# Two attentions' projections in one stage, beside head norm and rotary work in two fp32r passes

## The chip, the cores and the metric

The kernel runs on one core of a Trainium2 chip. The metric is the device time of one execution in microseconds, the median of several runs. The engines are PE (TensorE, matrix multiplication; PEld is its weight load), DVE (VectorE), ACT (ScalarE), POOL (GpSimd) and SP (SyncE, which issues the loads of weights).

## What is computed

A hybrid model of two blocks on 512 tokens of width 1024, in float32. The first block mixes a state-space branch, an RWKV branch and an HGRN branch. The second block has two layers; each mixes four branches of width 512. Those that matter here:

```python
y_a = mlstm_branch(aq, ak, av, ao, ag, a_conv_w, a_gate_bias, a_norm_g)
y_b = gqa_branch(bq, bk, bv, b_qnorm_g, b_knorm_g)
y_c = natten_branch(cq, ck, cv, c_rpb)
y_d = diff_branch(dq, dk, dv, d_lq1, d_lk1, d_lq2, d_lk2, d_subln_g, lambda_init)
...
# end of mlstm_branch, per head of 128
h = (h - mu) * lax.rsqrt(var + EPS)
h = h * norm_g
return h * jax.nn.sigmoid(o)
...
# gqa_branch: 8 query heads and 2 key heads of 64
q = rms_norm(q, qn_g); k = rms_norm(k, kn_g)
q = axial_rope(q, ang_r, ang_c) * (B_DH ** -0.5)
k = axial_rope(k, ang_r, ang_c)
```

Branch D ends with a norm over heads of 128 too, and so does HGRN in the first block.

## The kernel before

Activations lie transposed: 128 features on the partitions, 512 tokens along them, a matrix of 1024 features as 8 tiles. A product in float32 accuracy is made of three fp32r passes (`three_passes`, lines 555 to 557): weight and activation are each split into a high part, rounded to fp32r, and a low part, the rest. Weights stream in chunks of at most 128x1024. For every chunk SP loads it (four slots ahead), ACT makes its high part (L478), DVE its low part (L484), both into two slots, and PE multiplies. `run_ahead` makes ACT and DVE prepare chunk p+2 as soon as PE has used chunk p.

The program is a row of stages. Each is one `nc.Block()` with a stream for each engine, and no engine enters the next stage before all have left the last (the branches at L882 or L1338 are such borders). `project` multiplies k.xn by a list of weight matrices; ACT takes each finished tile out of PSUM (L1000), and for a tokens job four tiles at the end (L1008). Work of another kind runs beside it: a side object has one generator per engine, and `next(side_pieces)` runs its next piece behind each chunk, on PE right behind the chunk's matmuls, on ACT and DVE ahead of the preparation for the chunk after. What is left at the end runs in `list(side_pieces)`. `Together` advances two sides at once.

Per layer three stages stand in a row: the mLSTM's (branch A), then `project` of B's q, k, v (6 tiles) with `HeadNorm` of A beside it, then `project` of D's q, k (8 tiles) and v (four token chunks) with `DiffSetup` (lambda, a distance bias on POOL) and `Rotary` (norm and rotation of B's q and k) beside it. Behind them comes `project_beside` for C.

`HeadNorm` works on tile m: PE sums the tile with a matrix of ones (L3286) for the mean if it centres, DVE subtracts (L3322), ACT squares (L3306), PE sums the squares (L3293), ACT takes Sqrt (L3312), DVE the reciprocal (L3328), and multiplies by weight and inverse (L3332), then by the gate (L3336). `Rotary` squares (L3834), sums over pairs of 64 (L3860), Sqrt (L3839), reciprocal (L3880), scaling (L3882), a matmul with the turning matrix (L3866), three DVE operations with sine and cosine (L3887 to L3890), and at the end doubles the keys (L3871, L3850). All these constant matmuls are plain fp32: 8 per layer in A's norm, 12 in the rotary work, 4 per layer in D's norm (beside the mixing of C, in `gated_products`, where gate chunks are 1024 wide and value chunks 512), and 4 in HGRN's norm (beside `w_mix_ssm`, with chunks of 1024 alone). That makes 52.

## Time and profile before

| | us |
|---|---|
| median of 3 runs (3898.14 to 3909.04) | 3904.27 |
| the profiled execution | 3907.71 |
| its span, first to last instruction | 3905.5 |
| PE busy | 3674.9 (94%) |
| DVE busy | 2036.4 (52%) |
| ACT busy | 1528.7 (39%) |
| mean granted clock of TensorE | 0.969 |

The span is divided by engine: busy is time with an instruction at work. PE's matmul records overlap, so the distance from one start to the next is what a matmul costs, not its own length. The granted clock is the share of 2.4 GHz that TensorE got, 0.5 being 1.2 GHz.

### The profile page before, as it was taken

The numbers are of one execution on the slowest core, as the hardware profiler recorded it, in microseconds if no ns is written. First come the engines' busy times: TensorE is split into PE (matmuls) and PEld (weight loads), VectorE is DVE, ScalarE is ACT, GpSimd is POOL, SyncE is SP. The second block draws the span as 40 slices with busy tenths as digits, with TensorE's granted clock in tenths as the row PEclk, the third lists the DMA queues.
The fourth block names the chain that finished last, engine by engine and source line by source line (L and its number), as shares of the span: only waits on it lengthen the run. The fifth ranks groups of instructions, "written<-read, shape, count | busy, mean of one in ns | idle before, by whom it ended". The sixth has DMA issues, their size and how long they took to land. (4 is left out here: it accounts for less than half of the span.)

```text
span 3905.5 us, 51947 instructions
## 1 busy us (share of the span) xinstructions
PE 3674.9 (94%) x20468; PEld 2855.8 (73%) x20468; DVE 2036.4 (52%) x3128; ACT 1528.7 (39%) x2404; POOL 400.5 (10%) x353
## 2 busy tenths in 40 slices
PE   7898889969999999889999999999889999999998
PEld 5456777758878887666777788887666777788887
DVE  4879665584443334656545553333565555544332
ACT  4464432543343334333444333323433454333322
POOL 0018233000011110310000001100010000001100
PEclk9899989979999999999999999999999999999999
DMA  3011001203232232112212232232212112232232
GB/s 111 22 41 60 7 2 61 71 12 120 90 100 97 97 95 84 49 52 67 68 49 99 88 105 94 97 96 88 65 40 74 56 59 98 86 103 92 97 95 78
DMA packets 83486, 289.31 MB, mean 74 GB/s; under 512 B 9168, under 2 KB 9296, under 8 KB 82000
## 3 DMA queue, kind: packets, MB, share of 16 engines
q1 hardware_dynamic: 82848, 283.68, 22.7%
q8 instruction: 142, 2.33, 0.2%
q10 hardware_dynamic: 432, 2.78, 0.2%
q14 instruction: 64, 0.52, 0.0%
HBM read 284.32 MB, written 2.10 MB: 73 GB/s over the span
## 5 line engine op out<-in xcount | busy, mean ns | idle before, releaser
L484 DVE TENSOR_TENSOR weights_lo_r<-raw_weights,weights_hi_r 128x1024 fp32r<-128x1024 f32 (+2 forms) x554 | 639.4, 1154 | 1310.7 <-ACT weights_hi_r L478 1310.4
L478 ACT ACTIVATE weights_hi_r<-raw_weights 128x1024 fp32r<-128x1024 f32 (+2 forms) x554 | 547.1, 988 | 1396.6 <-PE ps L557 1323.1
L556 PE MATMUL ps<-xn_r,weights_hi_r 128*128 128x512 f32 x2688 | 1057.3, 393 | 0.0
L555 PE MATMUL ps<-xn_hi,weights_hi_r 128*128 128x512 f32 x1632 | 681.6, 418 | 65.6 <-PEq L882 23.4
L557 PE MATMUL ps<-xn_hi,weights_lo_r 128*128 128x512 f32 x1632 | 646.7, 396 | 0.0
L556 PEld LDWEIGHTS ps<-xn_r,weights_hi_r 128*128 128x128 f32 x2688 | 511.9, 190 | 112.7 <-issue 12.0
L555 PE MATMUL ps<-y_r,weights_hi_r 128*128 128x512 f32 x1200 | 473.8, 395 | 8.0 <-DVE weights_lo_r L484 5.9
L557 PE MATMUL ps<-y_r,weights_lo_r 128*128 128x512 f32 x1200 | 470.0, 392 | 0.0
L555 PEld LDWEIGHTS ps<-xn_hi,weights_hi_r 128*128 128x128 f32 x1632 | 313.0, 192 | 168.2 <-issue 82.9
L557 PEld LDWEIGHTS ps<-xn_hi,weights_lo_r 128*128 128x128 f32 x1632 | 312.3, 191 | 69.0
L555 PEld LDWEIGHTS ps<-y_r,weights_hi_r 128*128 128x128 f32 x1200 | 227.3, 189 | 61.3 <-issue 13.2
L557 PEld LDWEIGHTS ps<-y_r,weights_lo_r 128*128 128x128 f32 x1200 | 227.4, 190 | 47.6
L555 PE MATMUL ps<-y_hi,weights_hi_r 128*128 128x512 f32 x576 | 230.4, 400 | 2.1 <-PEq L1126 1.9
L557 PE MATMUL ps<-y_hi,weights_lo_r 128*128 128x512 f32 x576 | 224.7, 390 | 0.0
L556 PE MATMUL ps<-y_r,weights_hi_r 128*128 128x512 f32 x528 | 209.2, 396 | 0.0
L555 PE MATMUL ps<-hidden_hi,weights_hi_r 128*128 128x512 f32 x528 | 206.4, 391 | 1.0 <-PEq L4210 1.0
L557 PE MATMUL ps<-hidden_hi,weights_lo_r 128*128 128x512 f32 x528 | 205.5, 389 | 0.0
L556 PE MATMUL ps<-hidden_r,weights_hi_r 128*128 128x512 f32 x528 | 205.5, 389 | 0.0
L1483 POOL TENSOR_TENSOR y<-y 128x512 f32<-128x512 f32 x18 | 23.3, 1293 | 1674.6 <-ACT y L1472 1674.6
L4307 POOL TENSOR_TENSOR y<-y 128x512 f32<-128x512 f32 x63 | 81.3, 1291 | 611.7 <-ACT y L4264 611.7
L555 PEld LDWEIGHTS ps<-y_hi,weights_hi_r 128*128 128x128 f32 x576 | 108.2, 188 | 29.6 <-issue 4.0
L557 PEld LDWEIGHTS ps<-y_hi,weights_lo_r 128*128 128x128 f32 x576 | 108.1, 188 | 23.1
(552 smaller groups left out, 5224.9 us busy)
## 6 DMA issues: line engine op xcount, KB each, us to landing
raw_weights<-in_w_ffn_dram SPq DMA_DIRECT2D x132, 512.0 KB, 3.7
raw_weights<-in_w_down_dram SPq DMA_DIRECT2D x48, 512.0 KB, 3.5
raw_weights<-in_w_out_dram SPq DMA_DIRECT2D x24, 512.0 KB, 3.5
raw_weights<-in_w_down_dram SPq DMA_DIRECT2D x24, 384.0 KB, 3.1
raw_weights<-in_w_hgrn_dram SPq DMA_DIRECT2D x16, 512.0 KB, 3.5
raw_weights<-in_w_mix_ssm_dram SPq DMA_DIRECT2D x16, 512.0 KB, 3.7
raw_weights<-in_w_a_qk_dram SPq DMA_DIRECT2D x16, 512.0 KB, 3.5
raw_weights<-in_w_mix_a_dram SPq DMA_DIRECT2D x16, 512.0 KB, 3.5
```

The lines of the kernel that those rows point to most:

```text
L478: act.activation(self.k.w_hi[:, g % 2, 0:chunk.width], self.k.raw[:, slot, 0:chunk.width], ACT.Copy)\
L484: dve.tensor_tensor(self.k.w_lo[:, g % 2, 0:chunk.width], self.k.raw[:, slot, 0:chunk.width], self.k.w_hi[:, g % 2, 0:chunk.width].bitcast ...
L555: pe.matmul(out, w_hi, x_hi, start=start, stop=False)
L556: pe.matmul(out, w_hi, x_lo, start=False, stop=False)
L557: return pe.matmul(out, w_lo, x_hi, start=False, stop=stop)
L1483: pool.tensor_tensor(self.sums[:, n, :], self.sums[:, n, :], self.sq[:, kinds * (m % 2) + n, :], ALU.add)\
L4307: pool.tensor_tensor(gate[:, s, :], gate[:, s, :], rstd, ALU.mult).then_inc(gate_scaled, 1)
```

## The change

- `two_passes` takes the place of the fp32 matmuls with constants: the constant is exact in fp32r, the other operand is split into high and low part, and two fp32r matmuls add up. Constants are rounded once by ACT copies (`sums_r`, `consts_r`).
- In `HeadNorm` and `Rotary` ACT squares twice (float32 and rounded to fp32r) and DVE subtracts the two; where y or q and k are the operand, ACT copies the high part and DVE subtracts.
- Sqrt and DVE's reciprocal become Ln and Exp(-0.5 x) on ACT, in place.
- A's norm is a piece later where it centres (`late`).
- B's and D's projections are one `project`, with A's norm, the rotary work (from piece 6 on, keys first) and `DiffSetup` (from piece 1 on) beside it. The rotary work uses the norm's buffers; its tensor side waits for the norm's last root before its first piece.
- A's gate o lies in y_b, and not in a buffer of its own.

```diff
+        act.wait_ge(self.more_in, 16)
+        at = k.rounded("turn", "dup")
+        act.activation(k.consts_r[:, at], k.consts[:, at], ACT.Copy)
...
+def two_passes(pe, out, exact, hi, lo):
+    pe.matmul(out, exact, hi, start=True, stop=False)
+    return pe.matmul(out, exact, lo, start=False, stop=True)
...
 class HeadNorm(Nothing):
...
     def tensor(self, pe):
+        k, w = self.k, self.work
+        for p in range(self.tiles + 2 + self.late):
+            m = p - self.late
+            if self.centre and 0 <= m < self.tiles:
+                pe.wait_ge(self.part_lo, m + 1)
+                if m >= 2:
+                    pe.wait_ge(self.centred, m - 1)
+                two_passes(pe, bank(k.ps, 4 + m % 2), self.over, w.hi[:, m % 2, :], w.lo[:, m % 2, :])\
+                    .then_inc(self.mean_done, 1)
+            m = p - 2 - self.late
+            if m >= 0:
+                pe.wait_ge(self.square_lo, m + 1)
+                if m >= 2:
+                    pe.wait_ge(self.root, m - 1)
+                two_passes(pe, bank(k.ps, 6 + m % 2), self.over, w.sq_hi[:, m % 2, :], w.sq_lo[:, m % 2, :])\
+                    .then_inc(self.summed, 1)
+            yield
...
     def scalar(self, act):
+        if self.rounds:
+            act.activation(k.sums_r[:, :], k.consts[:, k.rounded("ones", "pair")], ACT.Copy)
+        for p in range(self.tiles + 2 + self.late):
             m = p
             if self.centre and m < self.tiles:
                 if m >= 2:
-                    pe.wait_ge(self.centred, m - 1)
-                pe.matmul(bank(k.ps, 4 + m % 2), self.over, self.y[:, m, :], start=True, stop=True)\
-                    .then_inc(self.mean_done, 1)
-            m = p - 2
-            if m >= 0:
-                pe.wait_ge(self.squared, m + 1)
-                if m >= 2:
-                    pe.wait_ge(self.root, m - 1)
-                pe.matmul(bank(k.ps, 6 + m % 2), self.over, self.sq[:, m % 2, :], start=True, stop=True)\
-                    .then_inc(self.summed, 1)
-            yield
-
-    def scalar(self, act):
-        k = self.k
-        for p in range(self.tiles + 2):
-            m = p - 1
+                    act.wait_ge(self.mean_done, m - 1)
+                act.activation(w.hi[:, m % 2, :], self.y[:, m, :], ACT.Copy).then_inc(self.part_hi, 1)
+            m = p - 1 - self.late
             if 0 <= m < self.tiles:
                 if self.centre:
                     act.wait_ge(self.centred, m + 1)
                 if m >= 2:
                     act.wait_ge(self.summed, m - 1)
-                act.activation(self.sq[:, m % 2, :], self.y[:, m, :], ACT.Square).then_inc(self.squared, 1)
-            m = p - 2
+                act.activation(w.sq[:, m % 2, :], self.y[:, m, :], ACT.Square).then_inc(self.squared, 1)
+                act.activation(w.sq_hi[:, m % 2, :], self.y[:, m, :], ACT.Square).then_inc(self.squared, 1)
+            m = p - 2 - self.late
             if m >= 0:
+                rt = w.rt[:, m % 2, :]
                 act.wait_ge(self.summed, m + 1)
                 if m >= 2:
                     act.wait_ge(self.scaled, m - 1)
-                act.activation(self.rt[:, m % 2, :], bank(k.ps, 6 + m % 2), ACT.Sqrt, bias=self.eps,
+                act.activation(rt, bank(k.ps, 6 + m % 2), ACT.Ln, bias=self.eps,
                                scale=1.0 / (self.head * self.factor * self.factor)).then_inc(self.root, 1)
+                act.wait_ge(self.root, m + 1)
+                act.activation(rt, rt, ACT.Exp, scale=-0.5).then_inc(self.inverse, 1)
             yield
     def vector(self, dve):
+        for p in range(self.tiles + 3 + self.late):
+            m = p - self.late
+            if self.centre and 0 <= m < self.tiles:
                 dve.wait_ge(self.mean_done, m + 1)
                 dve.scalar_tensor_tensor(out=self.y[:, m, :], in0=bank(k.ps, 4 + m % 2), scalar=-1.0 / self.head,
                                          in1=self.y[:, m, :], op0=ALU.mult, op1=ALU.add).then_inc(self.centred, 1)
-            m = p - 3
+            m = p
+            if self.centre and m < self.tiles:
+                dve.wait_ge(self.part_hi, m + 1)
+                dve.tensor_tensor(w.lo[:, m % 2, :], self.y[:, m, :], w.hi[:, m % 2, :].bitcast(F32), ALU.subtract)\
+                    .then_inc(self.part_lo, 1)
+            m = p - 1 - self.late
+            if 0 <= m < self.tiles:
+                dve.wait_ge(self.squared, 2 * m + 2)
+                dve.tensor_tensor(w.sq_lo[:, m % 2, :], w.sq[:, m % 2, :], w.sq_hi[:, m % 2, :].bitcast(F32),
+                                  ALU.subtract).then_inc(self.square_lo, 1)
+            m = p - 3 - self.late
             if m >= 0:
-                rt = self.rt[:, m % 2, :]
-                dve.wait_ge(self.root, m + 1)
-                dve.reciprocal(rt, rt).then_inc(self.inverse, 1)
                 dve.wait_ge(self.inverse, m + 1)
                 if self.centre:
                     dve.wait_ge(self.centred, m + 1)
                 dve.scalar_tensor_tensor(out=self.y[:, m, :], in0=self.y[:, m, :], scalar=k.col(self.weight, m),
-                                         in1=rt, op0=ALU.mult, op1=ALU.mult).then_inc(self.scaled, 1)
+                                         in1=w.rt[:, m % 2, :], op0=ALU.mult, op1=ALU.mult).then_inc(self.scaled, 1)
...
 class Rotary(Nothing):
+    ORDER = (4, 0, 1, 2, 3)
...
     def scalar(self, act):
+        act.wait_ge(self.before.summed, self.before.tiles)
+        act.wait_ge(self.before.scaled, self.before.tiles - 1)
+        for p in range(self.pieces):
+            i, odd = divmod(p, 2)
+            if odd and i < N:
+                rt, key = w.rt[:, i % 2, :], self.ORDER[i] == 4
+                act.wait_ge(self.summed, i + 1)
+                if i < 2:
+                    act.wait_ge(self.before.scaled, self.before.tiles)
+                else:
+                    act.wait_ge(self.roped, 3 * (i - 1))
+                act.activation(rt, bank(k.ps, 4 + i % 2), ACT.Ln,
+                               bias=k.const("eps")[:, 0:1] if key else k.const("eps")[:, 3:4],
+                               scale=1.0 / 64 if key else 1.0).then_inc(self.root, 1)
+                act.wait_ge(self.root, i + 1)
+                act.activation(rt, rt, ACT.Exp, scale=-0.5).then_inc(self.inverse, 1)
+                if i == 0:
+                    act.wait_ge(self.v_turned, 1)
+                    act.activation(self.v_tok, bank(k.ps, 7).rearrange("p (j f) -> p j f", j=NT), ACT.Copy)\
+                        .then_inc(self.v_taken, 1)
...
     def tensor(self, pe):
+        pe.wait_ge(self.before.root, self.before.tiles)
+        pe.wait_ge(self.before.centred, self.before.tiles)
+        pe.wait_ge(self.tile_used, 6)
         for j in range(NT):
-            mm = pe.transpose(k.ps[:, 6, j * P:(j + 1) * P], self.v[:, j * P:(j + 1) * P], k.const("ident"))
+            mm = pe.transpose(k.ps[:, 7, j * P:(j + 1) * P], self.v[:, j * P:(j + 1) * P], k.const("ident"))
         mm.then_inc(self.v_turned, 1)
         yield
-        for m in range(5):
-            pe.wait_ge(self.squared, m + 1)
-            pe.matmul(bank(k.ps, 4 + m % 2), k.const("pair"), self.sq[:, m % 2, :], start=True, stop=True)\
-                .then_inc(self.summed, 1)
-            yield
-            pe.wait_ge(self.normed, m + 1)
-            if m == 0:
-                pe.wait_ge(self.v_taken, 1)
-            pe.matmul(bank(k.ps, 6 + m % 2), k.const("turn"), self.qk[:, m, :], start=True, stop=True)\
-                .then_inc(self.rotated, 1)
-            yield
-        pe.wait_ge(self.roped, 15)
-        for g in range(2):
-            pe.matmul(bank(k.ps, 4 + g), k.const("dup")[:, g * P:(g + 1) * P], self.qk[:, 4, :],
-                      start=True, stop=True).then_inc(self.doubled, 1)
+        for i in range(N + 1):
+            if i < N:
+                pe.wait_ge(self.square_lo, i + 1)
+                two_passes(pe, bank(k.ps, 4 + i % 2), k.const_r("pair"), w.sq_hi[:, i % 2, :], w.sq_lo[:, i % 2, :])\
+                    .then_inc(self.summed, 1)
+            if i:
+                pe.wait_ge(self.part_lo, i)
+                if i == 2:
+                    pe.wait_ge(self.v_taken, 1)
+                two_passes(pe, bank(k.ps, 6 + (i - 1) % 2), k.const_r("turn"), w.hi[:, (i - 1) % 2, :],
+                           w.lo[:, (i - 1) % 2, :]).then_inc(self.rotated, 1)
+            if i == N:
+                pe.wait_ge(self.root, N)
+                pe.wait_ge(self.part_lo, N + 1)
+                for g in range(2):
+                    two_passes(pe, bank(k.ps, 4 + g), k.const_r("dup")[:, g * P:(g + 1) * P], w.hi[:, N % 2, :],
+                               w.lo[:, N % 2, :]).then_inc(self.doubled, 1)
...
 def layer_branches(k, n, y, y_lo, early, product, opening):
...
+    o_gate = y_b
+    mlstm_branch(k, n, y_a, o_gate, norm, opening)
+    c_qk = k.sbuf(window, "c_qk", [P, 8, T], "right")
+    b_qk = k.sbuf(grouped_qkv, "b_qk", [P, 5, T], "right")
+    b_k2 = k.sbuf(grouped_qkv, "b_keys_twice", [P, 2, T], "right")
+    b_v = k.sbuf(grouped_qkv, "b_v", [P, NT, P], "right")
+    d_qk = k.sbuf(d_parts, "d_qk", [P, 8, T])
+    d_v = k.sbuf(d_parts, "d_v", [P, NT, 512])
+    lam, slope = k.sbuf(d_parts, "lambda", [P, 8]), k.sbuf(d_parts, "distance_bias", [P, D_HEADS, 896])
+    with ExitStack() as work:
+        v = k.sbuf(work, "b_v_rows", [P, 1, T], "right")
+        norm_a = HeadNorm(y_a, A_HEADS, P, f"a_norm{n}", k.const("eps")[:, 0:1], o_gate, centre=True)
+        rotary = Rotary(n, b_qk, b_k2, v[:, 0, :], b_v[:, :, :], 6, norm_a)
+        project(k, [(f"w_b_q{n}", b_qk[:, 0:4, :], 1.0), (f"w_b_k{n}", b_qk[:, 4:5, :], 1.0), (f"w_b_v{n}", v, 1.0),
+                    (f"w_d_q{n}", d_qk[:, 0:4, :], 0.125), (f"w_d_k{n}", d_qk[:, 4:8, :], 1.0)], k.xn,
+                tokens=(f"w_d_v{n}", d_v), beside=Together(Together(norm_a, rotary), DiffSetup(n, lam, slope)))
```

How the instructions stand now at three places. ACT beside A's norm in layer 0, one chunk's worth (L1000 or L1009 takes a tile, L478 or L487 makes a weight's high part), before:

```order
L478 ACTIVATE weights_hi_r_50<-raw_weights 128x1024 [waits chunk_used,weights_in_2]
L1000 ACTIVATE b_qk<-ps 128x512 [waits chunk_used]
L3306 ACTIVATE head_norm_work<-y 128x512 [waits e_ready_2071,ssm_scaled_3786]
L3312 ACTIVATE head_norm_work<-ps,consts 128x512 [waits e_ready_2071]
L478 ACTIVATE weights_hi_r_50<-raw_weights 128x1024 [waits chunk_used,weights_in_3]
```

The same place now:

```order
L487 ACTIVATE weights_hi_r_50<-raw_weights 128x1024 [waits chunk_used,weights_in_2]
L1009 ACTIVATE b_qk<-ps 128x512 [waits chunk_used]
L3339 ACTIVATE parts_hi<-y 128x512 [waits tile_used_7029]
L3346 ACTIVATE squares<-y 128x512 [waits tokens_used_7030]
L3347 ACTIVATE squares_hi<-y 128x512
L3354 ACT_TABLE_LOAD
L3354 ACTIVATE roots<-ps,consts 128x512 [waits sig_ready_7025]
L3357 ACT_TABLE_LOAD
L3357 ACTIVATE roots<-roots 128x512 [waits f_ready_7026]
L487 ACTIVATE weights_hi_r_50<-raw_weights 128x1024 [waits chunk_used,weights_in_3]
```

Five more instructions stand between two weight parts, two of them table loads.

PE at the border between B's and D's projections in layer 0, before:

```order
L557 MATMUL ps<-xn_hi,weights_lo_r_51 128x512
L3293 MATMUL ps<-head_norm_work,consts 128x512 [waits factor_ready_2072,ssm_normed_3787]
L882 UNCONDITIONAL_BRANCH
L924 UNCONDITIONAL_BRANCH [waits barrier_Pool_Activation_PE_DVE_SP_release]
L555 MATMUL ps<-xn_hi,weights_hi_r_50 128x512 [waits parts_ready]
```

Now (f_ready_7026 is the semaphore that the norm's Ln counts up):

```order
L566 MATMUL ps<-xn_hi,weights_lo_r_51 128x512
L3289 MATMUL ps<-squares_hi,sums_r 128x512 [waits f_ready_7026,exped_7024]
L3290 MATMUL ps<-squares_r_14623,sums_r 128x512
L3938 MATMUL ps<-consts,b_v_rows 128x128 [waits rest_ready_8006,tokens_used_7030,f_ready_7026]
L3938 MATMUL ps<-consts,b_v_rows 128x128 x3
L564 MATMUL ps<-xn_hi,weights_hi_r_50 128x512 [waits parts_ready,rest_ready_8006]
```

The border is gone; v is turned right behind the norm's last sum (which stands a chunk later than B's last tile), and waits for the norm's root.

ACT beside D's norm in layer 0, from one gate to the next, before:

```order
L1058 ACTIVATE gate<-ps 128x512 [waits chunk_used]
L3306 ACTIVATE head_norm_work<-y 128x512
L3312 ACT_TABLE_LOAD
L3312 ACTIVATE head_norm_work<-ps,consts 128x512 [waits source_ready_164]
L478 ACTIVATE weights_hi_r_50<-raw_weights 128x512 [waits chunk_used,weights_in_0]
L3306 ACTIVATE head_norm_work<-y 128x512 [waits source_ready_164]
L3312 ACTIVATE head_norm_work<-ps,consts 128x512 [waits source_ready_164]
L478 ACTIVATE weights_hi_r_50<-raw_weights 128x1024 [waits chunk_used,weights_in_1]
L1058 ACT_TABLE_LOAD [waits dt_steps_173]
L1058 ACTIVATE gate<-ps 128x512 [waits chunk_used]
```

Now, from the 512 wide weight part on:

```order
L487 ACTIVATE weights_hi_r_50<-raw_weights 128x512 [waits chunk_used,weights_in_0]
L3346 ACTIVATE squares<-y 128x512 [waits scanned_176]
L3347 ACTIVATE squares_hi<-y 128x512
L3354 ACT_TABLE_LOAD
L3354 ACTIVATE roots<-ps,consts 128x512 [waits scanned_176]
L3357 ACT_TABLE_LOAD
L3357 ACTIVATE roots<-roots 128x512 [waits squared_166]
L487 ACTIVATE weights_hi_r_50<-raw_weights 128x1024 [waits chunk_used,weights_in_1]
L1067 ACTIVATE gate<-ps 128x512 [waits y_ready_1166,chunk_used]
L3346 ACTIVATE squares<-y 128x512 [waits scanned_176]
```

The gate (a Tanh) lost its table load, since Exp stands ahead of it; each of the two pieces between the gates got two.

## Rows read from the trace of the kernel before

**Rows 1.** The page's part 1: busy time, share of the span, instructions.

```profile
PE 3674.9 (94%) x20468; PEld 2855.8 (73%) x20468; DVE 2036.4 (52%) x3128; ACT 1528.7 (39%) x2404; POOL 400.5 (10%) x353
```

**Rows 2.** Windows, both layers' joined stretch: PE, PEld, DVE, ACT, POOL, clock, DMA, GB/s.

```profile
1682.70:1823.30 140.60, 122.94 (x478) 91.98 (x479) 74.21 (x62) 43.73 (x61) 10.88 (x4) 0.94 0.22 68
2874.50:3012.10 137.60, 121.32 (x479) 90.62 (x479) 73.76 (x62) 43.73 (x61) 9.80 (x4) 0.95 0.21 69
```

**Rows 3.** Timeline of PE, layer 0: start, length, instruction, idle before and releaser.

```profile
1721.79 1.02 PE L3293 MATMUL ps<-head_norm_work,consts 128*128 128x512 f32 x2
...
1732.67 0.77 PE L555 MATMUL ps<-xn_hi,weights_hi_r 128*128 128x512 f32 x1 [9.85 <-PEq L882]
...
1743.05 0.59 PE L4103 MATMUL ps<-lambda,consts 128*128 128x2 f32 x2 [3.27 <-DVE lambda L4092]
...
1760.48 1.13 PE L3866 MATMUL ps<-b_qk,consts 128*128 128x512 f32 x2 [1.81 <-DVE b_qk L3882]
```

**Rows 4.** Timeline of DVE while PE is idle at the border, layer 0.

```profile
1722.71 3.34 DVE L3328 RECIPROCAL head_norm_work<-head_norm_work 128x512 f32<-128x512 f32 x1
...
1727.49 3.34 DVE L3328 RECIPROCAL head_norm_work<-head_norm_work 128x512 f32<-128x512 f32 x1
...
1731.65 0.69 DVE L3336 TENSOR_TENSOR y<-y,o_gate 128x512 f32<-128x512 f32 x1
```

**Rows 5.** Timeline of PE around one fp32 sum (L3293), layer 0.

```profile
1715.22 0.39 PE L557 MATMUL ps<-xn_hi,weights_lo_r 128*128 128x512 f32 x1
1715.45 1.02 PE L3293 MATMUL ps<-head_norm_work,consts 128*128 128x512 f32 x2
...
1716.54 0.40 PE L556 MATMUL ps<-xn_r,weights_hi_r 128*128 128x512 f32 x1
```

**Rows 6.** Timeline of ACT, Ln (L4258) and Exp (L4261) of another stage.

```profile
1151.55 1.28 ACT L4258 ACT_TABLE_LOAD   x1
...
1153.55 1.28 ACT L4261 ACT_TABLE_LOAD   x1
...
1155.49 1.28 ACT L4264 ACT_TABLE_LOAD   x1
```

**Rows 7.** Timeline of ACT in one chunk beside A's norm, layer 0.

```profile
1709.46 0.58 ACT L1000 ACTIVATE b_qk<-ps 128x512 f32<-128x512 f32 x1
1709.94 0.62 ACT L3306 ACTIVATE head_norm_work<-y 128x512 f32<-128x512 f32 x1
1710.46 0.68 ACT L3312 ACTIVATE head_norm_work<-ps,consts 128x512 f32<-128x512 f32 x1
```

**Rows 8.** Timelines of PE and ACT beside D's norm, layer 1.

```profile
3343.98 0.47 PE L555 MATMUL ps<-xn_hi,weights_hi_r 128*128 128x512 f32 x1 [1.84 <-PEq L1338]
...
3371.52 1.12 PE L3293 MATMUL ps<-head_norm_work,consts 128*128 128x512 f32 x2
...
3381.60 0.47 PE L555 MATMUL ps<-xn_hi,weights_hi_r 128*128 128x512 f32 x1 [0.76 <-DVE weights_lo_r L484]
...
3358.00 1.06 ACT L478 ACTIVATE weights_hi_r<-raw_weights 128x1024 fp32r<-128x1024 f32 x1 [4.33 <-PE ps L557]
3358.97 0.58 ACT L1058 ACTIVATE gate<-ps 128x512 f32<-128x512 f32 x1
```

**Rows 9.** Timelines of PE and ACT at the end of D's projections, layer 0.

```profile
1819.46 1.88 PE L3871 MATMUL ps<-b_qk,consts 128*128 128x512 f32 x4
...
1821.59 1.12 ACT L3850 ACTIVATE b_keys_twice<-ps 128x512 f32<-128x512 f32 x2
...
1823.31 0.47 PE L555 MATMUL ps<-xn_hi,weights_hi_r 128*128 128x512 f32 x1 [1.97 <-PEq L882]
```

**Rows 10.** An idle of PE elsewhere, and windows behind three idles (clock third from the end).

```profile
1562.20 0.77 PE L555 MATMUL ps<-y_r,weights_hi_r 128*128 128x512 f32 x1 [2.96 <-DVE weights_lo_r L484]
...
1562.00:1569.00 7.00, 6.80 (x17) 5.38 (x18) 6.79 (x10) 0.00 (x0) 0.00 (x0) 0.55 0.27 75
1732.60:1739.60 7.00, 6.93 (x24) 5.49 (x24) 1.60 (x1) 1.06 (x1) 6.05 (x3) 0.79 0.50 150
1743.00:1753.00 10.00, 9.95 (x33) 7.88 (x33) 0.00 (x0) 0.99 (x3) 1.50 (x1) 0.69 0.19 52
```

More of the change, by code:

```diff
@@ L306, in const, with rounded, const_r @@
         return self.consts[0:rows, a:b]
+    def rounded(self, first, last):
+        return slice(self.const_at[first][0], self.const_at[last][1])
+    def const_r(self, name):
+        if name in ("ones", "pair"):
+            return self.sums_r[:, 0:P] if name == "ones" else self.sums_r[:, P:2 * P]
+        return self.consts_r[:, self.rounded(name, name)]
     def col(self, name, j=0, rows=P):
@@ L3261, with __init__ @@
+def two_passes(pe, out, exact, hi, lo):
+    pe.matmul(out, exact, hi, start=True, stop=False)
+    return pe.matmul(out, exact, lo, start=False, stop=True)
 class HeadNorm(Nothing):
-    def __init__(self, y, tiles, head, weight, eps, gate, factor=1.0, centre=False, work=None):
+    def __init__(self, y, tiles, head, weight, eps, gate, factor=1.0, centre=False, rounds=False):
+        self.work, self.rounds = None, rounds
         self.y, self.tiles, self.head, self.weight, self.eps = y, tiles, head, weight, eps
-        self.gate, self.factor, self.centre, self.work = gate, factor, centre, work
+        self.gate, self.factor, self.centre = gate, factor, centre
+        self.late = 1 if centre else 0
@@ L3270, in open @@
     def open(self, k, ctx):
         self.k = k
-        work = self.work if self.work is not None else k.sbuf(ctx, "head_norm_work", [P, 4, T])
-        self.sq, self.rt = work[:, 0:2, :], work[:, 2:4, :]
-        self.over = k.const("ones") if self.head == P else k.const("pair")
-        (self.mean_done, self.centred, self.squared, self.summed, self.root, self.inverse, self.scaled,
-         self.normed) = semaphores(k, ctx, "mean_done centred squared summed root inverse scaled normed")
-    def tensor(self, pe):
-        k = self.k
-        for p in range(self.tiles + 2):
+        self.work = NormWork(k, ctx, self.centre)
@@ new lines, in open @@
+        self.over = k.const_r("ones" if self.head == P else "pair")
+        (self.part_hi, self.part_lo, self.mean_done, self.centred, self.squared, self.square_lo, self.summed, self.root,
+         self.inverse, self.scaled, self.normed) = semaphores(
+            k, ctx, "part_hi part_lo mean_done centred squared square_lo summed root inverse scaled normed")
+    def tensor(self, pe):
+        k, w = self.k, self.work
[15 more added lines that the diff above has]
+            yield
@@ L3829, in scalar @@
     def scalar(self, act):
[L3830 to L3845 removed]
+        k, w, N = self.k, self.before.work, len(self.ORDER)
@@ L3852, in tensor @@
     def tensor(self, pe):
-        k = self.k
+        k, w, N = self.k, self.before.work, len(self.ORDER)
+        for _ in range(self.first):
+            yield
+        pe.wait_ge(self.before.root, self.before.tiles)
+        pe.wait_ge(self.before.centred, self.before.tiles)
+        pe.wait_ge(self.tile_used, 6)
         for j in range(NT):
-            mm = pe.transpose(k.ps[:, 6, j * P:(j + 1) * P], self.v[:, j * P:(j + 1) * P], k.const("ident"))
+            mm = pe.transpose(k.ps[:, 7, j * P:(j + 1) * P], self.v[:, j * P:(j + 1) * P], k.const("ident"))
@@ L4101, in tensor @@
     def tensor(self, pe):
+        for _ in range(self.FIRST):
+            yield
         pe.wait_ge(self.products, 1)
@@ L4109, in scalar @@
     def scalar(self, act):
+        for _ in range(self.FIRST):
+            yield
         act.wait_ge(self.dots, 1)
```

140 lines of the change are left out of this document (76 added, 64 removed).

## The prediction

> **What bounds the kernel now.** I read the busy shares first: TensorE (PE) works 94% of the span, no other engine above 52% [rows 1]. So a microsecond counts only if TensorE waits in it, runs at its lower clock, or works longer than it must. Then I looked at the two stages that the change joins, once per layer, from the first matmul of B's projections to the first of the stage behind D's: 140.5 us in layer 0 and 137.7 in layer 1 [rows 2]. TensorE is busy for 122.9 of the first 140.6.
>
> The timeline of TensorE around the border of the two stages says where the rest lies. B's last work there ends at 1722.8, and the next matmul begins at 1732.67: 9.85 us idle, with a branch (L882) as the releaser, which is a stage's end, not a tensor [rows 3]. VectorE's (DVE) own rows say what the stage's end waited for: three reciprocals of the head norm, 3.34 us each, the last behind 1727.49, and the gate product at 1731.65 [rows 4]. D's stage then idles 3.27 us more before the lambda matmul, since its first piece needs a product that VectorE makes late [rows 3]. After both idles TensorE runs at its lower level, 1.2 instead of 2.4 GHz: granted clock 0.79 over 7 us and 0.69 over 10 us [rows 10]. A stretch at mean clock c loses (1 - c) times its length: 1.5 and 3.1 us.
>
> **The change, part by part.**
>
> *Matmuls with constants.* An ordinary fp32r matmul of 512 columns takes 0.227 us from start to start. Between 1715.22 and 1716.54 stand two of these and one fp32 matmul with a constant, so the latter costs 1.32 - 0.45 = 0.87 [rows 5]. Two fp32r passes cost 0.46. Saved: 0.4 us for each of 52 such matmuls.
>
> *The joined stage, if TensorE never waited.* It issues 14 tiles of 24 matmuls and four token chunks of 24: 432 x 0.227 = 98.1 us. Seventeen pairs of passes (8 of norm A, 9 of the rotary work) add 7.8, lambda and the turning of v 0.65. The last rotation and the two doublings fall into the tail: in the kernel before, 3.85 us pass from the doublings' start (1819.46) to the next stage's first matmul, because ScalarE (ACT) takes out four tiles and then copies the doubled keys from 1821.59 [rows 9]. ScalarE has the same to do after the change, so 3.85 stays. Sum 110.4.
>
> *What ScalarE gets.* Instead of one Sqrt it now runs Ln and Exp for each tile, and the built program has a table load before each of them. The trace has this very sequence: load at 1151.55, next load at 1153.55, next at 1155.49, so a pair costs 3.94 us [rows 6]. Squares are made twice (0.52, and 0.64 if a load follows: 1.16), a tile is taken from PSUM in 0.48 [rows 7], a weight's high part in 0.96 [rows 8]. In chunks 3 to 5 ScalarE must do 0.96 + 0.48 + 1.16 + 3.94 = 6.5 us, in chunk 3 another 0.5 for the high part of y: 7.0. TensorE needs 24 x 0.227 plus one or two pairs, 5.9 to 6.4. ScalarE therefore falls behind.
>
> *Who waits for that.* Weight parts are made a chunk ahead, so a lag of 1 to 2 us there costs nothing. But the rotary piece behind chunk 6 makes TensorE wait for the fourth Ln of norm A before it turns v. With 0 at the first matmul, chunk 3 ends at 4 x 5.45 + 2 x 0.46 + 0.25 = 22.9, and chunk 6 with its sum at 42.0. ScalarE begins chunk 3's work at 23.2 and ends its rounds at 30.2, 36.7 and 43.2; then come high part, tile, table load and Ln: 0.96 + 0.48 + 2.0, to 46.6. TensorE waits 4.6 us. Behind TensorE's wait stands all of its queue: the next tile's 24 matmuls. Idles of 2.96, 3.27 and 9.85 us were each followed by the lower clock, costing 3.1, 3.1 and 1.5 us [rows 3, 10]; I take 2.3. The start of the rotary work (its first Ln waits for norm A's last scaling) costs perhaps 0.5. So the stage takes 110.4 + 4.6 + 2.3 + 0.5 = 117.8.
>
> *Stage gain.* 140.5 - 117.8 = 22.7 in layer 0, 137.7 - 117.8 = 19.9 in layer 1. The reciprocals go to nobody: VectorE gets subtractions of 0.7 us each for them, at most 4.6 us of a chunk, inside 6.
>
> *Norm D beside the mixing of C (once per layer).* A value chunk here has half the work, so the two chunks of a tile give TensorE only 8.2 us, against two pairs of Ln and Exp. With 0 at 3343.98, ScalarE starts the fifth weight part at 14.0 [rows 8]. Then: 0.96 + 0.48, squares 1.16, pair 3.94, to 20.5; 0.52, 1.16, 3.94, to 26.1; 0.96, 0.48 and the last squares 1.16, to 28.7; VectorE subtracts until 29.4. TensorE reached the fourth sum at 27.5 before (3371.52) and would reach it at 26.2 with three cheaper sums and a 0.17 us wait less. It waits 3.2 us. Without a fall of the clock the ninth chunk starts at 39.3, with it at 40.4; before it was 37.6 (3381.60). Cost 1.7 to 2.8 us, I take 2.5, twice: 5.0.
>
> *HGRN's norm.* Both chunks are full ones. ScalarE's last squares come out 0.2 us before TensorE wants them by the same working, so only the saving stays: 4 x 0.4 = 1.6. If that cover were missing it would cost about what a norm D costs.
>
> *Rest.* Rounding the constants (copies below 0.6 us on ScalarE, behind LoadX and in the first norm piece) lies beside full chunks: nothing. The gate o moves into y_b, a place and no time. POOL's distance bias, 10.9 us, moves to the head of the joined stage, where nobody reads it until the next one: nothing. The loads on SP's queue keep their order, and their distance to the use.
>
> Sum: 22.7 + 19.9 + 1.6 - 5.0 = 39.2 us. The profiled execution took 3907.7 us, 3.4 above the median of the runs, 3904.3; the stages' times do not depend on that, so I subtract from the median: 3865.1.
>
> **A rule of the skill against a row.** The pair of Ln and Exp has two loads in the trace, each with 1.28 us and 0.02 us around it [rows 6]. The Trainium skill (ScalarE: Activation LUTs, What ACT_TABLE_LOAD costs) counts a drain with every switch, about 2.66 us in all. By that a pair would be 6.7 us, most of the 30 pairs would lie open, and an estimate by that page puts the kernel some 70 us later, near 3935; the row disagrees. The same page (Table sets: the hidden batching unit) has Ln and Exp in one set with a single load; the rows show two. The first of these rules stands beside the third rival below, the second beside the fourth.
>
> **Rivals.**
>
> *No waits on TensorE.* If ScalarE's operations overlap more than the rows show, the root wait, the clock's fall and norm D's wait vanish: 2 x 6.9 + 2 x 3.5 = 21 us more gain, 3844. For it: such waits hang on a few microseconds. Against it: the wait for the fourth root is at least one load and one Ln behind the tile's copy, even without any lag.
>
> *The wait moves into the rotary work.* Its chain per tile is longer now: square, low part, sum, Ln, Exp, scaling, high part, low part, turn. Before, the turning matmul waited 1.81 us for VectorE with one tile, little with others [rows 3]. If each of five tiles waits 0.6 to 1.8 us per layer, 6 to 18 us go: 3871 to 3883. Against it: by the rows ScalarE's odd pieces end 0.7 us before the next chunk does.
>
> *Slower: table loads bind the stage.* Thirty pairs have 60 loads. If all lay open and each cost over 1.29 + 0.65 us, the gain would be gone; at twice the row, 60 x 1.3 = 78 us more, 3943. Against it: every load row is 1.28, and ScalarE has work for only two thirds of the joined stage.
>
> *One load for Ln and Exp.* ScalarE's rounds would be 1.29 shorter, so no lag: root wait 3.2 instead of 4.6, norm D's wait under 1 and no fall of the clock there. About 8 us more gain: 3857. Against it: the built program places two.
>
> *It does nothing.* The idle at the border could reappear at the joined stage's end. VectorE's last piece is three operations of 0.7 us, shorter than ScalarE's tail, which speaks against it: 3904.
>
> **How the numbers follow.** Forecast 3865 (3856 to 3873): 0.62. No waits: 0.12. Rotary waits: 0.19. Slower: 0.03. One load: 0.01. Nothing: 0.03. The range takes in most of the two neighbours, 3846 to 3882, and leaves some 0.18 out. A difference under 0.3% (12 us) can't be told from none; faster by more 0.94, within 0.03, slower 0.03.
>
> **What would show it.** Right: no idle near 10 us between B's and D's projections; joined stages near 118 us; one TensorE idle of 4 to 5 us before the transposes of v, ended by ScalarE's Ln, and one near 3 us before norm D's fourth sum, both followed by a granted clock under 1; two fp32r passes at 0.227 us each. Wrong: table load and Ln rows longer than here, TensorE idles before the turning matmuls of each tile, an idle at the end of the joined stage, or the fp32r passes at more than 0.25 us.

## The result, and the profile after

The changed kernel takes 3865.5 us (median of 3 runs, 3862.3 to 3868.3) against 3904.3: ratio 0.990, 95% interval 0.988 to 0.992. Forecast was 3865 (3846 to 3882), faster with chance 0.94. The profiled execution's span fell from 3905.5 to 3863.6, by 41.9 us. Of all executions behind this document one fell far out, 7381 us for the kernel two_recip below, whose median of 3930.5 is 3929.0 without it. Part 1 of its page, to be read beside [rows 1]:

```profile
PE 3649.7 (94%) x20468; PEld 2856.7 (74%) x20468; DVE 1968.5 (51%) x3148; ACT 1628.6 (42%) x2528; POOL 401.1 (10%) x353
```

TensorE is still 94% busy; VectorE gave 68 us away, ScalarE took 100. The windows of the joined stage, first matmul to the first of the next stage, answer to [rows 2] (PE, PEld, DVE, ACT, POOL, then clock, DMA share, GB/s):

```profile
1682.00:1798.60 116.60, 110.07 (x478) 90.03 (x478) 56.35 (x72) 79.12 (x104) 9.95 (x4) 0.99 0.26 82
2850.00:2967.90 117.90, 111.36 (x479) 91.02 (x479) 55.84 (x72) 79.12 (x104) 11.56 (x4) 0.97 0.25 81
```

By the starts themselves the stage took 140.5 and 137.7 us and takes 116.5 and 117.8. TensorE's timeline there has no idle near 10 us any more ([rows 3] had 9.85, 3.27 and 1.81). What is left is one wait before v is turned, the same in both layers, and the tail:

```profile
1682.09 0.47 PE L564 MATMUL ps<-xn_hi,weights_hi_r 128*128 128x512 f32 x1 [0.94 <-PEq L3540]
...
1728.75 1.12 PE L3938 MATMUL ps<-consts,b_v_rows 128*128 128x128 f32 x4 [4.43 <-ACT roots L3354]
...
1798.63 0.47 PE L564 MATMUL ps<-xn_hi,weights_hi_r 128*128 128x512 f32 x1 [2.00 <-PEq L891]
```

The wait is for norm A's fourth Ln. ScalarE's timeline shows why it is late: it has no gap from chunk 3 on, and each pair of roots has its two table loads, as in [rows 6]:

```profile
1725.17 1.04 ACT L487 ACTIVATE weights_hi_r<-raw_weights 128x1024 fp32r<-128x1024 f32 x1
1726.12 0.58 ACT L1009 ACTIVATE d_qk<-ps 128x512 f32<-128x512 f32 x1
1726.71 1.28 ACT L3354 ACT_TABLE_LOAD   x1
1728.01 0.69 ACT L3354 ACTIVATE roots<-ps,consts 128x512 f32<-128x512 f32 x1
1728.71 1.28 ACT L3357 ACT_TABLE_LOAD   x1
1730.01 0.63 ACT L3357 ACTIVATE roots<-roots 128x512 f32<-128x512 f32 x1
```

Windows of the 20 us before the wait and the 10 us after it, layers 0 and 1. ACT works 19.80 of 20 us; then the clock is 0.85 and 0.71, a loss of 1.5 and 2.9 us:

```profile
1708.00:1728.00 20.00, 16.32 (x73) 13.17 (x71) 10.53 (x16) 19.80 (x24) 0.00 (x0) 1.00 0.24 79
1728.70:1738.70 10.00, 9.95 (x40) 8.32 (x41) 2.11 (x4) 4.50 (x6) 0.00 (x0) 0.85 0.11 46
2896.60:2906.60 10.00, 9.92 (x34) 8.14 (x35) 0.88 (x2) 3.98 (x7) 0.00 (x0) 0.71 0.14 47
```

Norm D beside C's mixing, to be read beside [rows 8] (first matmul, fourth sum, ninth chunk; layer 0): 39.65 us from the first to the ninth chunk, where it was 37.6 before.

```profile
2132.16 0.47 PE L564 MATMUL ps<-xn_hi,weights_hi_r 128*128 128x512 f32 x1 [1.84 <-PEq L1347]
...
2161.45 0.56 PE L3289 MATMUL ps<-squares_hi,sums_r 128*128 128x512 f32 x1 [2.07 <-DVE squares_r L3376]
...
2171.81 0.47 PE L564 MATMUL ps<-xn_hi,weights_hi_r 128*128 128x512 f32 x1
```

### The profile page after: what moved, and what is told of

Same layout as the page of the kernel before. It is cut to its first block and busy times, and to the rows that moved or that the text cites. A ratio compares the mean times of both kernels' runs of the same rounds, so it can differ in the third digit from the quotient of the medians.

```text
span 3863.6 us, 52128 instructions
## 1 busy us (share of the span) xinstructions
PE 3649.7 (94%) x20468; PEld 2856.7 (74%) x20468; DVE 1968.5 (51%) x3148; ACT 1628.6 (42%) x2528; POOL 401.1 (10%) x353
## 3 DMA queue, kind: packets, MB, share of 16 engines
q8 instruction: 142, 2.33, 0.3%
## 5 line engine op out<-in xcount | busy, mean ns | idle before, releaser
L487 ACT ACTIVATE weights_hi_r<-raw_weights 128x1024 fp32r<-128x1024 f32 (+2 forms) x554 | 546.8, 987 | 1256.5 <-PE ps L566 1201.7
L564 PE MATMUL ps<-xn_hi,weights_hi_r 128*128 128x512 f32 x1632 | 669.5, 410 | 44.2 <-DVE xn_r L559 12.1
```

What stands on the lines that cost most here:

```text
L487: act.activation(self.k.w_hi[:, g % 2, 0:chunk.width], self.k.raw[:, slot, 0:chunk.width], ACT.Copy)\
L564: pe.matmul(out, w_hi, x_hi, start=start, stop=False)
```

## The experiments

In this section a "root wait" is TensorE's wait for norm A's fourth Ln (or Sqrt) before it turns v, a "rotary sum" is the sum over pairs of 64 in `Rotary`, and "the parts" are the high and low parts that the two passes need. The theory from the reading: the border's idle went with the join and the reciprocals together, TensorE's sums gave some 20 us more, and ScalarE's lag took part of it back at the root wait and in norm D. The rivals: one of the three parts did all of it; or the lag is not ScalarE's. Table of all runs (stages in us from the profile, layers 0 and 1; "norm D" is first to ninth chunk, taken where it starts at full clock):

| kernel | joined stage(s) | norm D | median us | ratio to before (95%) |
|---|---|---|---|---|
| before | 140.5, 137.7 | 37.6 | 3904.3 | |
| changed | 116.5, 117.8 | 39.7 | 3865.5 | 0.990 (0.988 to 0.992) |
| two_stages | 129.3, 130.9 | 39.3 | 3890.7 | 0.997 (0.996 to 0.999) |
| recip | 127.6, 127.4 | 39.7 | 3892.3 | 0.996 (0.995 to 0.998) |
| two_recip | 145.9, 149.5 | 39.7 | 3930.5 | 1.008 (1.006 to 1.010) |
| full_sums | 122.2, 120.6 | 39.3* | 3881.9 | 0.995 (0.993 to 0.997) |
| plain | 122.2, 122.1 | 37.7 | 3869.5 | 0.993 (0.991 to 0.994) |
| no_ln | 112.2, 112.2 | 35.8 | 3851.3 | 0.987 (0.986 to 0.989) |
| v_bank6 | 112.7, 112.6 | 39.7 | 3856.6 | 0.989 (0.987 to 0.990) |
| rec_nc | 116.7, 117.9 | 39.7 | 3866.8 | 0.991 (0.988 to 0.993) |
| dve_sq | 115.5, 115.9 | 37.7* | 3858.3 | 0.989 (0.986 to 0.991) |
| best | 111.5, 111.5 | 39.7 | 3858.0 | 0.987 (0.985 to 0.990) |
| best2 | 111.5, 111.5 | 37.7 | 3849.8 | 0.987 (0.986 to 0.989) |

The runs were taken in three groups, each on another chip: two_stages, full_sums, v_bank6 and no_ln; then recip, rec_nc, dve_sq and best; then plain, two_recip and best2. The kernel before took 3903.6, 3905.6 and 3899.0 us beside them. Stages that no edit touches differ between two profiles too: the one from 1504 to 1628 us by up to 6 us, the one from 427 to 641 us by up to 10 (214.8 us at clock 0.90 in the changed kernel, 222.4 at 0.85 in full_sums). So stage lengths say more than medians here. The star: both layers' norm D began at clock 0.72 over 6 us, and the 1.6 us that this costs are taken off (40.9 and 39.3 as read; the first sum starts 15.4 us in, elsewhere 13.8). For two_stages the column has layer 0; layer 1 took 39.7.

### Join, roots and passes

**two_stages.** B's and D's projections apart again; `Rotary` starts with D's and has buffers of its own:

```diff
-        rotary = Rotary(n, b_qk, b_k2, v[:, 0, :], b_v[:, :, :], 6, norm_a)
...
+        rotary = Rotary(n, b_qk, b_k2, v[:, 0, :], b_v[:, :, :], 0, None)
...
+                beside=norm_a)
+        project(k, [(f"w_d_q{n}", d_qk[:, 0:4, :], 0.125), (f"w_d_k{n}", d_qk[:, 4:8, :], 1.0)], k.xn,
+                tokens=(f"w_d_v{n}", d_v), beside=Together(DiffSetup(n, lam, slope), rotary))
```

> The changed kernel with its join undone: B's and D's projections are two stages again (norm A beside the first, the rotary work and the lambda beside the second), but the sums stay two fp32r passes and the roots stay Ln and Exp. Theory: the join itself is worth only the idles at the border less the idles that it brings. Without reciprocals the tail of norm A behind the last matmul is last sum, Ln, Exp, scaling, gate product, some 5.3 us in place of 9.85; the lambda idle of 3.3 comes back; the root wait of 4.43 and its lower clock go. Both stages together 120 to 123 us in layer 0 instead of 116.5, the kernel at 3872 to 3878. Rival 1: the join is the main part of the gain; then the border shows near 10 us of idle again and the kernel takes 3885 or more. Rival 2: the join brings nothing once the reciprocals are gone; 3868 or less.

Rival 1 came nearest: 3890.7. The rows at the border, layer 0:

```profile
1721.60 0.50 PE L3289 MATMUL ps<-squares_hi,sums_r 128*128 128x512 f32 x1 [2.72 <-DVE squares_r L3376]
...
1730.54 0.76 PE L564 MATMUL ps<-xn_hi,weights_hi_r 128*128 128x512 f32 x1 [8.21 <-PEq L891]
...
1742.14 0.38 PE L4203 MATMUL ps<-lambda,consts 128*128 128x2 f32 x2 [3.27 <-DVE lambda L4190]
```

I had reckoned 5.3 us of tail from idle engines. But ScalarE is late there too: its third pair is still ahead of the fourth, whose load starts at 1724.78, 2.4 us behind the last sum, and the gate product ends at 1730.2. Without the join ScalarE's lag becomes idle time of the border; with it, only the part up to the fourth Ln is waited for. The join is worth 12.7 and 13.1 us, as the changed kernel has it: the extra piece of norm A (`late`) stays in two_stages, so the norm's last sum and all of the fourth root stand behind B's last tile, where the kernel before had that sum right behind the tile's matmuls. How much of the border's 2.72 and 8.21 us comes from that piece no run separates.

**recip.** Join and passes stay, Sqrt and reciprocal return:

```diff
-                act.activation(rt, bank(k.ps, 6 + m % 2), ACT.Ln, ...
-                act.activation(rt, rt, ACT.Exp, scale=-0.5)...
+                act.activation(rt, bank(k.ps, 6 + m % 2), ACT.Sqrt, ...
+                dve.reciprocal(w.rt[:, m % 2, :], w.rt[:, m % 2, :])...
```

> The changed kernel with Sqrt and VectorE's reciprocal again in place of Ln and Exp, in all head norms and in the rotary work; the join and the two passes stay. ScalarE loses both table loads and the Exp, VectorE gets 3.34 us per tile and has then 7.8 us to do in a chunk of norm A in which TensorE needs 5.9 to 6.4. Theory: ScalarE's lag is what cost the joined stage its waits, and VectorE's new lag costs about as much there (2 to 4 us per layer), while norm D gets cheaper by some 3.2 us each: 3852 to 3866. Rival: the join only pays with Ln and Exp; TensorE then idles more than 5 us in each joined stage for VectorE's low parts and the rotary work waits for each tile: 3870 or more.

The rival held. The root wait fell to 2.33 us, but the rotary work now waits for VectorE at every tile. TensorE's rows, then VectorE's ahead of the second of them:

```profile
1748.68 0.50 PE L3289 MATMUL ps<-squares_hi,sums_r 128*128 128x512 f32 x1 [2.04 <-DVE squares_r L3983]
...
1764.37 0.50 PE L3289 MATMUL ps<-squares_hi,sums_r 128*128 128x512 f32 x1 [1.68 <-DVE squares_r L3983]
...
1807.51 0.51 PE L3289 MATMUL ps<-parts_hi,consts_r 128*128 128x512 f32 x1 [2.47 <-DVE parts_lo L3987]
```

```profile
1758.44 1.23 DVE L493 TENSOR_TENSOR weights_lo_r<-raw_weights,weights_hi_r 128x1024 fp32r<-128x1024 f32 x1 [5.61 <-ACT weights_hi_r L487]
1759.58 3.35 DVE L3975 RECIPROCAL roots<-roots 128x512 f32<-128x512 f32 x1
...
1762.96 0.75 DVE L3977 SCALAR_TENSOR_TENSOR b_qk<-b_qk,cols,roots 128x512 f32<-128x512 f32 x1
1763.63 0.69 DVE L3983 TENSOR_TENSOR squares_r<-squares,squares_hi 128x512 fp32r<-128x512 f32 x1
```

VectorE idles 5.61 us there and still is late: the low part of the squares, new with the passes, stands behind a reciprocal in its order. I had priced load, not order. Norm D did not get cheaper either; rec_nc below shows why.

**two_recip.** Both undone:

> The changed kernel with the join and the Ln/Exp both undone: two stages, Sqrt and reciprocal, but sums in two passes. With two_stages and recip it fills the square of join and roots. Theory: the two parts are substitutes in the tail and complements in the rows: undone alone each cost 25 to 27 us; both undone VectorE's reciprocals stand in the border (10 us idle there) and before the rotary sums (five waits of 1.7 to 2 us per layer), 140 to 143 us for both stages, 3905 to 3920. Rival: the two remove the same idle, so undoing both costs little more than one: 3890 to 3900.

Slower than the kernel before, above even my range. The border's idle is now

```profile
1733.47 0.76 PE L564 MATMUL ps<-xn_hi,weights_hi_r 128*128 128x512 f32 x1 [13.86 <-PEq L891]
```

and each rotary sum but the first waits 1.7 to 1.9 us. Three reciprocals of norm A lie in this idle, where the idle of the kernel before held two (at 1722.71 and 1727.49 in [rows 4], and not the three that the prediction names), since norm A is a piece later. So the passes with what came along (norm A a piece later, the rotary work's new order, o in y_b), in two stages and with the old roots, lose 31 us against the kernel before; how the passes and the new order share that loss no run tells. 65 us separate this kernel from the changed one, more than join (25) and roots (27) undone singly add up to: each of these two edits is worth more with the other.

**full_sums.** The constants' matmuls are fp32 again, and all parts are still made:

```diff
-                two_passes(pe, bank(k.ps, 6 + m % 2), self.over, w.sq_hi[:, m % 2, :], w.sq_lo[:, m % 2, :])\
+                pe.matmul(bank(k.ps, 6 + m % 2), self.over, w.sq[:, m % 2, :], start=True, stop=True)\
```

> The changed kernel with the matmuls with constants as plain fp32 matmuls again, at the same places; the parts for them are still made, so ScalarE and VectorE do the same work. Theory: each of the 52 matmuls costs 0.41 us more on TensorE, 21 us, of which some 2 to 4 us fall into the root waits and norm D's waits, which shrink because TensorE comes later (three or four such matmuls stand ahead of each wait): 3882 to 3886. Rival: the passes save more than their own time, because ScalarE waits for the sums too; then the waits stay or grow and the kernel takes 3888 or more. Other rival: the waits hide most of it, 3876 or less.

3881.9 is the median that the theory had, but the stages give only some 9 us of its 16: 5.7 and 2.7 in the joined stages, 1.7 in HGRN's norm, less 0.4 in each norm D. The rest lies in stages that the edit doesn't touch (8 us in the one from 427 to 641 us alone), so the median hit by luck. The stage's rise in layer 0, 5.7, is 17 x 0.41 = 7.0 less what the root wait shrank (4.43 to 2.90). In layer 1 the rise is 2.7, since the clock did not fall behind the shorter wait. The other three matmuls of each layer lie in the tail, and cost nothing to be seen: the idle at its end is 0.94 in place of 2.00. So of 21 us on TensorE more than half vanish in its waits, their clock and the tail.

**plain.** As full_sums, and the parts are gone too:

```diff
-                act.activation(w.sq_hi[:, m % 2, :], self.y[:, m, :], ACT.Square).then_inc(self.squared, 1)
...
-                dve.tensor_tensor(w.sq_lo[:, m % 2, :], w.sq[:, m % 2, :], ...
```

> The changed kernel with plain fp32 matmuls for all constants again and, other than in full_sums, without the parts: no rounded squares, no high and low parts of y and qk. Join and Ln/Exp stay. This undoes the two passes as a whole. Theory: the passes' 21 us on TensorE are partly paid back, since the parts load ScalarE (0.52 to 1.0 us per tile) and VectorE, and their absence frees the waits. A chunk of norm A gives TensorE 7.2 us then, and ScalarE 5.9, so no lag: root wait 2 to 3 us, joined stage 119 to 121; norm D's ninth chunk at 38 us instead of 39.65. 3867 to 3874. Rival 1: the parts cost nobody anything, as full_sums gives it: 3879 to 3884. Rival 2: the passes bring nothing net: 3865 or less.

3869.5, in the forecast's range, though the joined stages came to 122.2 and 122.1, above its 119 to 121. This prices the passes as a whole: 5.6 and 4.3 us in the joined stages and 1.6 in HGRN's norm (four sums), less 1.9 in each norm D (37.7 without them, the time of before, though Ln and Exp are there). That is 7.7 us by the stretches, and 4 by the medians (9 if each median is taken from that of the kernel before beside it), of the change's 39, not 21. And it is little less than the 9 of full_sums, by the same stretches: the parts as such cost about 2 us, and what takes most of the 21 away is that TensorE comes sooner and waits longer, 4.43 us in place of 2.83 for the fourth root, and in norm D.

### ScalarE's lag

**no_ln.** Ln becomes Identity, so the program computes no roots and no table is loaded between the operations:

> The logarithm is left out: where the changed kernel takes Ln of a sum of squares, in the head norms and in the rotary work, this one takes the same tile through Identity, so the same number of ScalarE operations of the same size stay and the table loads between Ln and Exp go. Theory: the waits of the changed kernel come from ScalarE, and of its time the two loads per pair (2.6 us of 3.94) are what is too much. Then the root wait falls from 4.43 to under 1.5 us, norm D's wait from 2.07 to nothing, both with their lower clock: 15 to 21 us, 3844 to 3850. Rival: the waits hang on the order of the pieces rather than on the loads; then they stay above 2 us and the kernel is above 3856.

3851.3: the stages lie at 112.2, norm D at 35.8, with 0.29 us of wait at its fourth sum. The root wait stays at 1.82 us, what the order itself leaves (ScalarE makes a weight's high part and copies the tile, then comes the operation in Ln's place, without a gap); my 1.5 was a little low, as the gain of 14 against 15 to 21.

**v_bank6.** v is turned in PSUM bank 6, for which the third root is enough:

```diff
-        pe.wait_ge(self.before.root, self.before.tiles)
+        pe.wait_ge(self.before.root, self.before.tiles - 1)
...
                 if i == 2:
+                    pe.wait_ge(self.before.root, self.before.tiles)
```

> The changed kernel with v turned in PSUM bank 6 instead of 7, so that TensorE waits for norm A's third root there and not for the fourth; the fourth is waited for two pieces later, before the rotation that writes bank 7. Theory: the root wait of 4.43 us is taken away with its fall of the clock (1.5 and 2.9 us), but ScalarE's lag behind it stays: the next sum, of the first rotary tile, waits for ScalarE's squares and VectorE's subtraction, some 2 us. The kernel gains 4 to 8 us, 3857 to 3861. Rival 1: nothing waits in its place, the whole 13 us come, 3852. Rival 2: the lag is ScalarE's and the wait only moves on in full, 3863 to 3867, with an idle of 4 us before the first rotary sum.

The root wait is gone and a smaller one stands at the first rotary sum, in both layers, with the clock whole behind it:

```profile
1735.32 0.50 PE L3289 MATMUL ps<-squares_hi,sums_r 128*128 128x512 f32 x1 [2.23 <-DVE squares_r L3985]
```

```profile
1735.20:1745.20 10.00, 9.88 (x43) 8.17 (x44) 4.96 (x7) 8.00 (x12) 0.00 (x0) 1.00 0.22 57
```

The stages gain 3.9 and 5.2: 2.2 of wait, and the 1.5 and 2.9 of clock. That is 9.1, a little over my 4 to 8, because I had not given the clock back in full.

**dve_sq.** The full squares of the head norms move to VectorE:

```diff
-                act.activation(w.sq[:, m % 2, :], self.y[:, m, :], ACT.Square).then_inc(self.squared, 1)
...
+                    dve.tensor_tensor(w.sq[:, m % 2, :], self.y[:, m, :], self.y[:, m, :], ALU.mult)
```

> The changed kernel with the full squares of the head norms made by VectorE (a product of 0.7 us) instead of ScalarE (0.52 us each); the rounded squares stay on ScalarE, the rotary work is as it was. Theory: ScalarE's rounds of 7.0, 6.5 and 6.4 us become 6.5, 5.9 and 5.9, so it keeps up with TensorE and only the chain of the fourth root stays: root wait 2.3 to 3.2 us instead of 4.43, norm D's wait about 0.5 instead of 2.07. 5 to 9 us, 3857 to 3861. Rival: VectorE's longer row (5.3 us of each chunk) hands its low parts over later and gives the gain back: root wait as before or small waits at each sum, 3864 or more.

Root wait 3.24, stages 115.5 and 115.9, as the theory had it. In norm D there are two waits, 0.62 and 1.15 us, in place of one of about 0.5, but the clock behind them is whole: 37.7 us in place of 39.7.

**rec_nc.** Sqrt and reciprocal in norm D and HGRN's norm alone (the edit of recip, if the norm doesn't centre):

> The changed kernel with Sqrt and reciprocal only in the norms without a mean, norm D (twice) and HGRN's norm; norm A and the rotary work keep Ln and Exp. Theory: norm D's wait for its fourth squares is ScalarE's lag from the pairs of table loads. With one Sqrt instead the wait of 2.07 us goes and so does the slow stretch behind it; start to ninth chunk falls from 39.65 to about 36.4 (before the change 37.6, less three cheaper sums): 6 to 7 us in all, 3858 to 3860. Rival: the lag is in the weights' parts and the squares; the wait stays above 1.5 us and the kernel takes 3863 or more.

My theory fell: no gain. In layer 1 norm D takes 39.7 us, the same as with Ln and Exp. The wait moved, from the fourth squares to VectorE's queue (layer 0):

```profile
2155.93 0.50 PE L3289 MATMUL ps<-squares_hi,sums_r 128*128 128x512 f32 x1 [1.71 <-DVE squares_r L3377]
...
2167.18 0.50 PE L564 MATMUL ps<-xn_hi,weights_hi_r 128*128 128x512 f32 x1 [2.34 <-DVE weights_lo_r L493]
```

VectorE's timeline has no gap from 2155.18 to the end of the reciprocal that starts at 2166.95, with three reciprocals of 3.35 in it; the low part of the weights that TensorE wants at 2167.18 is made between the last two. The second wait is the start of the ninth chunk, and what it does to the clock lies behind what the table's column takes in, in both layers (layer 0):

```profile
2167.10:2177.10 10.00, 9.92 (x37) 7.92 (x37) 7.07 (x6) 1.55 (x2) 0.00 (x0) 0.83 0.26 79
```

So this edit costs some 1.5 us more per norm D than the 39.7 shows: the whole stage takes 140.8 us in layer 1, where the changed kernel has 139.4. HGRN's norm takes 227.4 in place of 226.6. Together with plain (37.7) and no_ln (35.8) this says what norm D's loss is: the parts on top of either kind of root. Neither the loads alone nor the parts alone cost anything there: 37.7 is the time of before, and 35.8 that less four sums cheaper by 0.41.

**best.** v_bank6, VectorE's squares in norm A, Sqrt and reciprocal in D and HGRN:

> Three edits on the changed kernel at once: v is turned in bank 6 (the root wait is taken away), norm A's full squares come from VectorE, norm D and HGRN's norm take Sqrt and reciprocal. Theory: all of it is ScalarE's lag, so the gains add up: 9 us measured for bank 6, 6 to 7 for norm D, and 2 to 4 for the 2.2 us wait at the first rotary sum, which shrinks to about 1: 3845 to 3849. Rival: the edits remove the same wait twice; then no better than 3853.

The stages did what was forecast (111.5), norm D did not, for the reason just shown, and took 39.7 with the lower clock behind it; 3858.0, above the rival's 3853 too, though not by its cause. **best2** drops that third edit and takes VectorE's squares everywhere:

> The changed kernel with v turned in bank 6 and with the full squares of all head norms on VectorE; norm D keeps Ln and Exp (Sqrt and reciprocal had moved its wait to VectorE and brought nothing). Theory: joined stages at 111.5 us as in the last run, norm D's ninth chunk at 39.3: 12 to 13 us below the changed kernel, 3852 to 3855. Rival: the gain of the last run was partly from the reciprocals in HGRN's norm; then 3856 or more.

3849.8 us, some 16 below the changed kernel and 49 below the one before (which took 3899.0 beside it, so against the kernels before the step is 10); the stages give 15: stages 111.5, norm D 37.7 where I had said 39.3, because I had read dve_sq's time without seeing that it began at the lower clock. The wait at the first rotary sum is 1.06 us. Its four executions (3846.6 to 3851.4) all lie below the three of the changed kernel (3862.3 to 3868.3); the two ratios' intervals (0.986 to 0.989 and 0.988 to 0.992) just overlap.

## Why the prediction was right, step by step

- **Joined stage, 117.8 forecast:** 116.5 and 117.8. Less the root wait and the clock that makes 110.6 and 110.5 (forecast 110.4). The root wait is 4.43 (forecast 4.6, from ScalarE's rounds of 7.0, 6.5, 6.5; measured 6.96, 6.42, 6.41). The clock's 2.3, a middle of the costs seen and no working, were 1.5 and 2.9: right in the sum of both layers by luck. The 0.5 for the start of the rotary work is not to be seen on TensorE.
- **Gains 22.7 and 19.9:** 24.0 and 19.9.
- **Norm D, cost 2.5 each:** 2.0. The step that was mis-sized is the wait: 2.07, not 3.2. TensorE came later than I had it, by waits of 0.29 and 0.20 at two sums before. The clock fell behind it, as taken (0.76 over 7 us). The old wait of 0.76 ahead of the ninth chunk [rows 8] went too, which the prediction's working leaves standing. The terms (four sums cheaper by 1.6 in all, the old waits of 0.17 and 0.76 gone, 2.56 of waits, 1.7 of clock) give 1.7, so some 0.3 is left unexplained.
- **HGRN's norm, gain 1.6:** from the first chunk to the fourth sum, 37.29 became 36.04 with three sums cheaper, 1.25; no wait there.
- **Two passes at 0.46:** starts at 889.18 and 889.41, 0.23 apart.
- **Sum 39.2:** 41.9 between the two profiled spans, 38.8 between the medians. The edited stages alone give 41.6 (24.0, 19.9 and 1.8, less 1.9 and 2.2 for norm D's whole stages), so 3865.1 against 3865.5 is closer than the working was: the kernel before alone moved from 3899.0 to 3905.6 between the groups.
- **The rivals.** "No waits" needed ScalarE's operations to overlap; no_ln shows that without the loads it would have come to 3851, not 3844. "The wait moves into the rotary work" was wrong for this kernel and right for recip, where VectorE is what is waited for. "Table loads bind" was wrong: each is 1.28 us, as in the rows of before. "One load" was wrong: every pair has two. Of "it does nothing" nothing was seen: the tail is 2.00 us.

What the prediction did not see is how the gain divides. It priced the passes at 0.4 us for each of 52 matmuls, 21 us. By the stretches plain gives them 7.7 and full_sums 9: the rest comes back in waits that the prediction booked as terms of their own, as if the passes had no share in them, and this is why the sum came out. It also took the border's idle as the reciprocals' alone, while two_stages shows 8.21 us of it with none, behind a ScalarE that is late and with norm A a piece later.

## What to carry to other kernels

Where TensorE is the bound, price a cheaper matmul together with the waits behind it: if another engine is late, TensorE comes sooner and waits longer, and 21 us became 8. Then ask what the operands need of the other engines, and look for the place in the row where that work stands behind a long operation: an engine idle 5 us can still be late. Joining two stages paid here even though the engine that is late stays late, since its lag now ends before a single operation and not before everything. And ask of each wait which of several buffers it is for: one bank earlier was worth 9 us here.

## What the runs showed of the hardware

The length of TensorE's idle does not by itself say whether the granted clock falls to the lower level behind it. At the root wait it fell behind 4.43, 3.24 (dve_sq) and 2.83 us (plain) in both layers, behind 2.90 (full_sums) in layer 0 and not in layer 1, and not behind 2.33 (recip) or 1.82 (no_ln). Behind norm D's fourth sum, which waits 2.06 and 2.07 us in the two layers of two_stages, with the same instructions, it stayed whole in layer 0 and fell in layer 1:

```profile
2173.33:2180.33 7.00, 7.00 (x31) 5.80 (x32) 3.26 (x5) 6.91 (x8) 0.00 (x0) 1.00 0.36 115
3353.70:3360.70 7.00, 7.00 (x24) 5.60 (x25) 3.25 (x5) 6.90 (x9) 0.00 (x0) 0.76 0.34 112
```

Norm D's stage starts behind an idle of 1.84 us in every kernel here; the first 6 us after it were at full clock in the changed kernel, in both layers. In dve_sq they were at 0.72 in both, and in rec_nc so, layer 0 and layer 1:

```profile
2125.87:2131.87 6.00, 6.00 (x19) 4.77 (x20) 3.10 (x5) 2.71 (x5) 0.00 (x0) 0.72 0.43 134
3295.20:3301.20 6.00, 6.00 (x26) 4.96 (x27) 3.10 (x5) 2.89 (x6) 0.00 (x0) 1.00 0.45 131
```

v_bank6, which changes nothing in norm D, has the same pair: 0.72 in layer 0, where the changed kernel has 1.00, and 1.00 in layer 1. So with the same instructions and the same idle this comes and goes, 1.6 us each time. An idle of 2 to 3 us should be priced with and without it, and a stretch compared only with its clock beside it. What decides between the two stays open.
